# A decoder trunk's even mixer: another order for input blocks, conv taps, padded queries and two modulation groups

## What is computed

```python
z = h @ W['w_in_even'][e]                      # (520, 2568)
q, k, v, fl, a, b = jnp.split(z, cuts, axis=-1)   # 512 512 512 8 512 512
logf = log_sigmoid(fl + b_forget)
o_fox = fox_attend(e, q, k, v, logf)           # 8 heads of 64
u = a * sigmoid(b)                             # 512 channels
cv = depthwise_conv(concat([conv_buf, u]), width 31) + conv_b
cv = silu(group_norm(cv) * conv_norm_g + conv_norm_b)
out = concat([o_fox, cv]) @ W['w_out_even'][e]
```

## Time and profile before

| | us |
|---|---|
| median of 3 runs | 1890.92 |
| lowest and highest run | 1886.56, 1895.22 |
| the profiled execution | 1894.45 |
| its span, first to last instruction | 1892.3 |
| PE, DVE, ACT, POOL busy in the span | 1727.2, 896.7, 596.9, 198.2 |
| mean granted TensorE clock | 0.945 of full |

### The profile page before, as it was taken

How to read it: one execution, slowest core, us unless ns; L and a number is a source line. 1 busy time by engine, 2 the same in 40 slices (tenths; PEclk the granted TensorE clock), 3 DMA queues, 4 the chain that set the end, 5 groups by cost and what they waited for, 6 DMA issues and landing times.

```text
span 1892.3 us, 33709 instructions
## 1 busy us (share of the span) xinstructions
PE 1727.2 (91%) x13817; PEld 1561.8 (83%) x13817; DVE 896.7 (47%) x1470; ACT 596.9 (32%) x880; POOL 198.2 (10%) x172
## 2 busy tenths in 40 slices
PE   4798877889899999998999999999959899999997
PEld 3698744449899999998978788798629899999996
DVE  3429588764533233225517546347463533333234
ACT  2333234443432222223324333324322432222222
POOL 1006560001000000001001101001120100000001
PEclk7799767899999999998999999999979999999998
DMA  8946654546636237335323517225736133333321
GB/s 249 273 132 193 185 153 120 168 127 156 168 89 184 84 89 180 89 96 138 95 79 121 197 56 228 90 78 182 235 134 167 57 96 94 89 89 90 90 69 55
DMA packets 368714, 248.96 MB, mean 132 GB/s; under 512 B 9768, under 2 KB 338888, under 8 KB 368591
## 3 DMA queue, kind: packets, MB, share of 16 engines
q1 hardware_dynamic: 333716, 197.04, 37.0%
q0 software_dynamic: 9296, 33.82, 5.1%
q10 hardware_dynamic: 25587, 16.45, 2.9%
HBM read 224.05 MB, written 23.70 MB: 131 GB/s over the span
## 4 chain that ended last, share of the span: by engine, by line
PE 76%; DVE 11%; DMA 3%; ACT 3%; issue 2%; POOL 2%; SPq 1%; ACTq 1%; POOLq 0%; DVEq 0%
PE product L824 56%; PE product L839 6%; DVE CV L1904 2%; POOL sqa L2364 2%; DMA raw<-in_ada_w 2%; PE job L1269 2%; PE job L1252 1%; PE job L715 1%; PE job L1186 1%; DVE SC L1918 1%; PE job L1169 1%; PE product L1017 1%; DVE w_lo L1775 1%; PE job L774 1%; PE product L1112 1%
## 5 line engine op out<-in xcount | busy, mean ns | idle before, releaser
L824 PE MATMUL product<-H_hi,w_lo 128*128 128x260 f32 x2368 | 671.9, 284 | 3.2 <-ACT gate L1301 3.1
L824 PE MATMUL product<-H_hi,w_hi 128*128 128x260 f32 x2368 | 670.1, 283 | 0.0
L824 PE MATMUL product<-H_lo,w_hi 128*128 128x260 f32 x2368 | 669.6, 283 | 0.0
L824 PEld LDWEIGHTS product<-H_hi,w_lo 128*128 128x128 f32 x2368 | 447.0, 189 | 4.5 <-issue 2.5
L824 PEld LDWEIGHTS product<-H_lo,w_hi 128*128 128x128 f32 x2368 | 447.1, 189 | 1.4
L824 PEld LDWEIGHTS product<-H_hi,w_hi 128*128 128x128 f32 x2368 | 447.6, 189 | 0.0
L1775 DVE TENSOR_TENSOR w_lo<-raw,w_hi 128x1024 fp32r<-128x1024 f32 (+1 forms) x228 | 278.4, 1222 | 188.5 <-ACT w_hi L1301 187.9
L1301 ACT ACTIVATE w_hi<-raw 128x1024 fp32r<-128x1024 f32 (+1 forms) x228 | 234.9, 1037 | 254.5 <-PE product L824 188.4
L824 PE MATMUL product<-G_hi,w_lo 128*128 128x260 f32 x880 | 250.6, 285 | 2.8 <-DVE G_lo L1784 1.5
L824 PE MATMUL product<-G_hi,w_hi 128*128 128x260 f32 x880 | 249.8, 284 | 0.0
L824 PE MATMUL product<-G_lo,w_hi 128*128 128x260 f32 x880 | 249.6, 284 | 0.0
(11 more groups left out here) (329 smaller groups left out, 2175.0 us busy)
## 6 DMA issues: line engine op xcount, KB each, us to landing
spare<-in_ada_w SPq DMA_DIRECT2D x48, 512.0 KB, 7.3
raw<-in_w_in_odd SPq DMA_DIRECT2D x48, 512.0 KB, 3.9
raw<-in_w_ffn_gate SPq DMA_DIRECT2D x44, 512.0 KB, 4.2
raw<-in_w_ffn_up SPq DMA_DIRECT2D x44, 512.0 KB, 3.8
kp<-in_cache_k SPq DMA_DIRECT2D x64, 256.0 KB, 2.8
raw<-in_w_ffn_down SPq DMA_DIRECT2D x32, 512.0 KB, 4.7
st<-in_state_ret POOLq DMA_DIRECT2D x28, 512.0 KB, 4.7
out_ret_sample<-st POOLq DMA_DIRECT2D x28, 512.0 KB, 5.1
```

What stands on the lines that cost most here:

```text
L824: mm = pe.matmul(Gp[slot][:, c, 0:CH], w[:, j, k, :], x[:, k, cols], start=k == 0 and p == 0, stop=k == kt - 1 and p == 2)
```

## The change

It reorders the even mixer's work; nothing is computed otherwise.

- **Input blocks.** Channel tile 0's a and b blocks become blocks 0 and 1, the queries 2 to 5, the other a and b blocks 6 to 11. `qs` and `qb` move two blocks later (`QS_AT` 6, `QB_FROM` 8).
- **Taps.** 23 taps of channel tile 0 run in iterations 3 to 8, none in 9 to 14, one in each of 15 to 19; 12 more stand before the first four row maxima (`EARLY_TAPS`). Tiles 0 and 1 are done one tap after the other, each waiting for the one before; tiles 2 and 3 alternate as before. The taps end at step 28 instead of 30. Sample taps come one tile at a time (`SAMPLE_AT`).
- **Dots.** None in iteration 9 but two, then four an iteration instead of 3.5; 42 before the attention instead of 39, the rest in 8 steps instead of 9.
- **Padded queries.** Three buffers for each parity; the first three are made in iteration 19, and in step x the query of x + 5 is padded before the exponential of x + 4, not after the division.
- **The first scores.** TensorE makes scores 0 to 3 before the transposes `ks`, `vn` and `vs`; ACT evicts those after the first four exponentials.
- **Modulation groups 6 and 7.** Their site in the projection (`("in", 0)`: eight loads on SP, two site products, two turns) goes; groups 6 to 9 run as 16 `ada_block`s in steps 0 to 11, two a step from step 8 on (`ada_before`), loaded by ACT.
- **Buffers.** `wf_lo`, `rows_site` and `rows_late` move or change use.

```diff
 ADA_FIRST = 4
-ADA_MID = 8
+ADA_MID = 6
...
 ADA_LATE = 20
-RAW_GROUPS = (0, 1, 2, 3, 8, 9)
-SPARE_SITES = ((("norm", 0), 4), (("in", 0), 6), (("norm", 1), 10), (("gu", 0), 12), (("gu", 1), 14), (("gu", 2), 16),
+RAW_GROUPS = (0, 1, 2, 3, 6, 7, 8, 9)
+SPARE_SITES = ((("norm", 0), 4), (("norm", 1), 10), (("gu", 0), 12), (("gu", 1), 14), (("gu", 2), 16),
...
 SITE_OF = {name: (i + 1, first) for i, (name, first) in enumerate(SPARE_SITES)}
-Q_AT, AB_AT, K_AT, V_AT = 0, 4, 12, 16
-IN_COLUMNS = ([P * j for j in range(4)] + [c for j in range(4) for c in (1544 + P * j, 2056 + P * j)]
+Q_AT, K_AT, V_AT = 2, 12, 16
+AB_COLUMNS = [(1544 + P * j, 2056 + P * j) for j in range(4)]
+IN_COLUMNS = ([*AB_COLUMNS[0]] + [P * j for j in range(4)] + [c for pair in AB_COLUMNS[1:] for c in pair]
...
 def a_block(t):
-    return AB_AT + 2 * t
+    return 4 + 2 * t if t else 0
 def b_block(t):
-    return AB_AT + 2 * t + 1
-QS_AT, QB_FROM, CS_AT, CUM_AT, CUMT_AT = 4, 6, 14, 15, 17
+    return a_block(t) + 1
+QS_AT, QB_FROM, CS_AT, CUM_AT, CUMT_AT = 6, 8, 14, 15, 17
+A_TILE = {a_block(t): t for t in range(4)}
+B_TILE = {b_block(t): t for t in range(4)}
+SAMPLE_AT = {4: 0, 10: 1, 12: 2, 14: 3}
 def dots_before(m):
-    return sum(3 + i % 2 for i in range(9, m))
+    return min(m - 9, 1) * 2 + 4 * max(m - 10, 0) if m > 9 else 0
...
     return min(NPG, dots_before(20) + 3 * x)
-DOT_STEPS = 9
+DOT_STEPS = 8
+TAPS_AT = {3: 2, 4: 3, 5: 5, 6: 5, 7: 5, 8: 3, **{m: 1 for m in range(15, 20)}}
+IN_TAPS = sum(TAPS_AT.values())
+EARLY_TAPS, TAP_END = [IN_TAPS + i for i in (6, 8, 10, 12)], 28
+def taps_before_step(x):
+    done = EARLY_TAPS[-1] + 2 * min(x, DOT_STEPS)
+    late = 4 * CW - EARLY_TAPS[-1] - 2 * DOT_STEPS
+    return done + (late * min(x - DOT_STEPS, TAP_END - DOT_STEPS) // (TAP_END - DOT_STEPS) if x > DOT_STEPS else 0)
 def taps_before(m):
-    return sum(2 - i % 2 for i in range(10, m))
-TAP_END = 30
-def taps_before_step(x):
-    done, late = taps_before(20) + 2 * min(x, DOT_STEPS), 4 * CW - taps_before(20) - 2 * DOT_STEPS
-    return done + (late * min(x - DOT_STEPS, TAP_END - DOT_STEPS) // (TAP_END - DOT_STEPS) if x > DOT_STEPS else 0)
+    return sum(n for i, n in TAPS_AT.items() if i < m)
 LT_AT, CC_AT, MT_AT, MB_AT, EXP_AT, DN_AT, VALUES_AT = 2, 8, 10, 11, 12, 14, 15
-ADA_TURN_AT = {5: 8, 9: 9}
+ADA_TURN_AT = {5: 6, 9: 7, 11: 8, 13: 9}
+ADA_TAKE_AT = {4: 6, 8: 7, 10: 8, 12: 9}
+def ada_before(x):
+    return min(16, x + max(0, x - 8))
...
                     rows_of("qs", QT)
-                if QS_AT <= m < QS_AT + 2:
-                    site_products(("in", 0), only=(m - QS_AT,))
...
                     rows_out("kn", m - V_AT, KT)
-            rows_of("ks", KT)
-            pe.wait_ge(slot_act, in_a + 20)
-            for b in range(TB):
-                rows_out("vn", b, VT)
-            rows_of("vs", VT)
...
                 pe.wait_ge(qz_ready, x + 1)
-                pe.matmul(bank[:, 0:n], qz2[h % 2][x % 2][:], KT[:, h // 2, NB:NB + n], start=True, stop=False)
+                pe.matmul(bank[:, 0:n], qz2[h % 2][q % 3][:], KT[:, h // 2, NB:NB + n], start=True, stop=False)
...
                 scores(x)
+            rows_of("ks", KT)
+            pe.wait_ge(slot_act, in_a + 20)
+            for b in range(TB):
+                rows_out("vn", b, VT)
+            rows_of("vs", VT)
...
                     scores(x + TB)
-                if x < 8:
-                    ada_block(4 * ADA_MID + x)
+                for i in range(ada_before(x), ada_before(x + 1)):
+                    ada_block(4 * ADA_MID + i)
...
                 stage_out(("kn", b), P, 512, A["k_prompt"][0, 0, b * P:(b + 1) * P].rearrange("p h d -> p (h d)"))
+            def pad_queries(x):
+                h, q = x // TB, x % TB
+                rows_ = slice(HD * (h % 2), HD * (h % 2) + HD)
+                if x >= 3:
+                    wait_job(act, ("s", x - 3))
+                n.up(f(qz2[h % 2][q % 3][rows_, :], QT[rows_, h // 2, NB + q * P:NB + (q + 1) * P], ACT.Copy), qz_ready)
...
                     ahead(m + 2)
+                if m == 19:
+                    act.wait_ge(rows_zero, 2)
+                    for x in range(3):
+                        pad_queries(x)
...
                 product_done(m)
-                if AB_AT <= m < K_AT and m % 2 == 1:
-                    t = (m - AB_AT) // 2
+                if m in B_TILE:
+                    t = B_TILE[m]
...
                     n.up(f(halves(gate[:, t % 2, :]), slot(m), ACT.Sigmoid), slot_act)
-                elif AB_AT <= m < K_AT:
-                    n.up(f(halves(AT[:, (m - AB_AT) // 2, :]), slot(m), ACT.Copy), slot_act)
-                elif m < AB_AT:
-                    n.up(f(halves(QT[:, m, :]), slot(m), ACT.Copy, scale=FOX_SCALE), slot_act)
+                elif m in A_TILE:
+                    n.up(f(halves(AT[:, A_TILE[m], :]), slot(m), ACT.Copy), slot_act)
+                elif Q_AT <= m < Q_AT + 4:
+                    n.up(f(halves(QT[:, m - Q_AT, :]), slot(m), ACT.Copy, scale=FOX_SCALE), slot_act)
...
             stage_keys(TB - 1)
-            stage_out("ks", NB, 512, A["k_sample"][0, :, 0].rearrange("p h d -> p (h d)"))
-            for b in range(TB):
-                wait_job(act, ("vn", b))
-                n.up(f(VN[:, b, :], Jp[jobs.bank(("vn", b))][:, :], ACT.Copy), emptied["A"])
-                n.own(emptied["A"])
-                store(act, A["v_prompt"][0, 0, b * P:(b + 1) * P].rearrange("p h d -> p (h d)"), VN[:, b, :], v_stored)
-            stage_out("vs", NB, 512, A["v_sample"][0, :, 0].rearrange("p h d -> p (h d)"))
...
                 n.up(f(w, w, ACT.Copy, scale=ri[:, x:x + 1]), p_ready)
-            def pad_queries(x):
-                h, q = x // TB, x % TB
-                rows_ = slice(HD * (h % 2), HD * (h % 2) + HD)
-                if x % (2 * TB) >= 2:
-                    wait_job(act, ("s", x - 2))
-                elif x >= 2 * TB:
-                    wait_job(act, ("s", x - 2 * TB + 2))
-                n.up(f(qz2[h % 2][x % 2][rows_, :], QT[rows_, h // 2, NB + q * P:NB + (q + 1) * P], ACT.Copy), qz_ready)
-            act.wait_ge(rows_zero, 2)
             for x in range(TB):
-                pad_queries(x)
+                if x < 2:
+                    pad_queries(x + 3)
                 exps(x)
-            pad_queries(TB)
+            stage_out("ks", NB, 512, A["k_sample"][0, :, 0].rearrange("p h d -> p (h d)"))
+            for b in range(TB):
+                wait_job(act, ("vn", b))
+                n.up(f(VN[:, b, :], Jp[jobs.bank(("vn", b))][:, :], ACT.Copy), emptied["A"])
+                n.own(emptied["A"])
+                store(act, A["v_prompt"][0, 0, b * P:(b + 1) * P].rearrange("p h d -> p (h d)"), VN[:, b, :], v_stored)
+            stage_out("vs", NB, 512, A["v_sample"][0, :, 0].rearrange("p h d -> p (h d)"))
...
                        ACT.Copy), emptied["A"])
+                if x + TB + 1 < STEPS:
+                    pad_queries(x + TB + 1)
...
                     divide(x + 2)
-                if x + TB + 1 < STEPS:
-                    pad_queries(x + TB + 1)
-                if x in (4, 8):
-                    take_rows(ADA_MID + x // 4 - 1)
-                if 1 <= x < 5:
-                    load_ada(4 * ADA_MID + x + 3)
+                if x in ADA_TAKE_AT:
+                    take_rows(ADA_TAKE_AT[x])
+                for i in range(ada_before(x - 1), ada_before(x)) if x else ():
+                    if i + 4 < 16:
+                        load_ada(4 * ADA_MID + i + 4)
...
                 cw = vec[:, V_CW + w * 4 + t:V_CW + w * 4 + t + 1]
-                n.own(conv_step, back=1)
+                n.own(conv_step, back=1 if t >= 2 else 0)
...
                 n.up(o, conv_step)
-            taps = [(t, w) for p in range(2) for w in range(CW) for t in (2 * p, 2 * p + 1)]
+            taps = [(t, w) for t in range(2) for w in range(CW)] + [(t, w) for w in range(CW) for t in (2, 3)]
...
                     low_rows(qs2, "qs", 0)
-                if m in (7, 9, 11, 13):
-                    t = (m - 7) // 2
+                if m - 2 in B_TILE:
+                    t = B_TILE[m - 2]
...
                     n.up(v.tensor_tensor(US[:, t, :, CW - 1], AT[:, t, 0:NB], gate[:, t % 2, 0:NB], ALU.mult), u_ready)
-                if m == 9:
-                    for g in site_groups(("in", 0)):
-                        ada_mod(g)
-                    wait_job(dve, ("adr", site_groups(("in", 0))[1]))
-                    dve.wait_ge(pad_ready, 1)
-                    n.own(u_ready)
-                if m == 13:
...
                     for e in range(2):
-                        for i in range(2):
+                        for i in range(3):
...
                     low_rows(cum2, "cumT", 1)
-                if m >= 9:
-                    spread(range(dots_before(m), dots_before(m + 1)), range(taps_before(m), taps_before(m + 1)))
-                if m in (13, 14):
-                    for t in (2 * (m - 13), 2 * (m - 13) + 1):
```

(14 more changed lines are left out.)

24 lines of the change are left out of this document (5 added, 19 removed).

## The result

The changed kernel takes 1879.1 us in the median of six runs (1874.1 to 1885.6), the kernel before beside it 1890.6 (1886.5 to 1895.2): a ratio of 0.9945, 95% interval 0.9926 to 0.9964. Run once more unedited, it gave 0.9951 (0.9930 to 0.9972). It is faster by 0.5%, about 10.5 us, where 18 were forecast. The profiled execution took 1877.74 us, among the faster of its six, and the only profile of the kernel before took 1894.45, 3.5 us above that kernel's median, so the two spans differ by 16.5 us where the medians differ by 11.5.

A forecast was written before the change was run, and what follows sets the result against it. It took TensorE, then DVE, to bound the projection, DVE the early attention, value pages the later. -16.2 + 0.8 + 0.7 - 3 = -17.7 us on 1894.45 gave 1876.8, or 1873 on the median; 8-in-10 range 1861 to 1886.

The forecast's parts named there:

- Part 1: Projection, to the end of block 19: -16.2 us, bounds -16.7 and -3, from removed site products and the `lf` wait.
- the 0.5 us: End of block 15 in the projection: what remains of TensorE's wait for `lf`, put at 0.5 us.
- DVE's sum of 32.7 us: Blocks 10 to 15: splits, dots, gated products, sample taps and `lf` on DVE take 32.7 us, so `lf` comes at 175.6.
- GpSimd's own sum: Blocks 10 to 15: 22 products from 137.2 on, then a last dot and split, put `lf` between 173 and 186 us.
- my middle price of 1.74: GpSimd's products in the projection: 1.74 us each, top of the pace within a run, between 1.53 and 2.09.
- the rival on GpSimd's pace: Projection: products at 1.9 us each hold it, 42 of them ending at 217; 1883 us in all, chance 0.13.
- Part 2: Last projection block to first transpose of probabilities: 23.1 us against 22.3 today, +0.8, bounds -2.1 and +3.6.
- The lag: Behind block 19: DVE is free only 2.9 us later, at 207.5, because GpSimd must first make 42 products.
- Part 3: Attention steps 0 to 14, bounded by DVE: +0.7 us, bounds -3.4 and +7.8, from dots, taps, sums, `ada` blocks and loads.
- The sentence weighed against it: Loads in steps 7 to 10: ACT and SP transfers share 16 engines, giving an estimated +1 us for the 3 taken.
- Part 4: Attention steps 15 to 31: -3 us, bounds 0 and -9, from value pages nearer SP's pace and fewer taps.
- The other side: Rival, projection blocks 3 to 8: taps beside the queries pace TensorE, +8 us, 1899 in all; chance 0.07.

## Why the prediction was right, and where its steps failed

The direction and the range held; the size was right in no step that carried it, except by parts that offset each other.

**Part 1 fell short: -9.9 us in the profile compared, -8.4 on the mean of eight, for -16.2.** The two site products and their turns went, as priced: block 15 ended at 176.2, forecast 177.1. The step that failed is the 0.5 us that I took for what is left of the wait for `lf`, with nothing for what follows it: the wait was 3.3 us. I let DVE's sum of 32.7 us stand alone. From its split at 141.10 to the end of `lf` at 179.38 DVE took 38.3: its dots waited 4.8 us for products, and `lf` lasted 1.26 instead of 0.19. So `lf` came 3.8 us late. GpSimd's own sum missed it too, though not by its price: the 22 products began at 135.49, and the dot of the last ran at 174.07, 1.75 us each, next to my middle price of 1.74, by which my sum gives `lf` at 177.9 (137.2 + 22 x 1.74 + 2.4). But behind that dot I put 2.4 us, for a dot and a split. In my own order a sample tap and `lf` stand there as well, and the whole took 5.3.

The second half of the miss: I priced a short wait by its own length. A wait of 3.3 us left the sums at 4.40 and the next block at 8.1, much as the wait of 7.3 had the earlier trace rows; the clock was at half for 10.2 us instead of 13.7. With `lf` there in time, the run with one line moved ended block 19 where I had put it, but by errors that offset: block 15 ended 1.1 us sooner than I had it (176.05), and block 16 took 7.5 us instead of 5.76, without any wait. The time lies between the forecast and the rival on GpSimd's pace (1883), which had the right engine: 42 products took from 135.49 to 211.46, 1.81 each for its 1.9. But up to the end of block 19 they reach TensorE through `lf` alone: in the run with `lf` sooner they took 1.70 each (135.47 to 206.88), and TensorE was never idle there.

**Part 2's sum was right by chance** (23.3 for 23.1). The lag was 1.3 us and not 2.9, while one tap took 5.05 us and the others some 0.77, where three beside GpSimd were to cost 1.3 each. That nothing is gained from the removed pads held for the reason given: row maxima behind taps. (With `lf` sooner the lag was 2.9: the last dot ended at 207.6, block 19 at 204.7.) What I did not see is that taps, products and evictions can all leave this stretch, which then takes 6.2 us.

**Part 3** was forecast 0.7 up and came out 0.5 down and 0.7 up in the two profiles. Its terms were read from sums and not separated. TensorE waited for `raw` four times, 4.6 us in all for 3, at 0.9 to 1.4 each. The sentence weighed against it, from the Trainium skill, DMA: Bandwidth & Descriptors, section "Issuing engines are not separate DMA queues", would have made that 1 us, an estimate; the pair of 292.49 and 292.50 fits what it says of interleaving, and the total here lay above my figure.

**Part 4** gave 4.5 and 2.5 us for 3. Its cause stays open. The run that put 20 taps back shows that taps pay in the whole (5.9 us), but most of it before step 15: this stretch took 92.4 us there, against 88.7 to 91.2 in the profiles with the changed kernel's taps, and 88.9 in the run with 12 more taps in steps 8 to 27. The padded queries' place is excluded (88.7).

**The other side** fell as argued: five taps took 3.90 us in blocks 5 to 7, 0.78 each, against the 0.99 from which they would have paced TensorE, which stayed at 36.00 of 36. The Trainium skill, VectorE: DVE Perf Modes, section "The DRAIN you can't avoid", measured on copies that a semaphore between them costs nothing extra; with the interleaved taps' 0.66 that is an estimate of 3.3 us for the five, and the trace differs. (The section also says that an operation that nothing holds starts earlier, which I left out.)

**Open.** Row max 12 to 19 took 31.7 to 39.1 us in versions whose steps there are nearly alike. How soon the attention began does not order them: the first turns came at 231.5 and 231.2 us in the longest (37.6 and 39.1), and at 229.6 in the shortest, the run with `lf` sooner (31.7). TensorE's waits for `raw` are longest there (6.0 and 7.2 us; 2.9 to 5.2 in the others), but neither spreading the blocks nor holding the w_out loads shortened it for certain. In their profiles that stretch took back most of what the evictions had gained (3.0 to 4.5 of 5.3 us) and more than the hold on GpSimd had (4.6 to 6 for 3.6); the 6 us of `lf` sooner did show in the whole.

## What to carry to other kernels

When two engines feed one wait, follow the slower feeder's path to the end: what stands behind its last item counts (5.3 us here for 2.4), and the two engines' waits for each other come on top of either sum. A wait that was merely shortened kept most of the low clock behind it (10.2 us of 13.7), and 3.4 us of it were there without any wait. At a seam between two stages, look at what each engine does while another holds the path: here taps, evictions and products all stood in one gap of 23 us, and moving them a few steps on, together with `lf` one block sooner, was worth 18 us, more than the change itself.

## What the runs showed of the hardware

DVE instructions can be held by GpSimd products that run back to back, for longer than one of them: a tap of 0.75 us took 5.05, until 0.56 us behind the end of the third product, and a copy of 0.17 us took 4.43 to 4.55 in seven profiles, until the third product ended. With GpSimd held until the fourth row maximum, no DVE instruction of that stretch took longer than alone. In the profiles with the held copy only the indirect load ran on GpSimd when the copy began, so the load seems to hold it as well; no run shows the load without products behind it. Dots beside such products keep to 0.67 to 0.69 us. The Trainium skill, SBUF — State Buffer, section "Who interferes with whom", says that a VectorE instruction with two SBUF inputs contends with a GpSimd instruction that reads SBUF, that a copy can in a mode that uses both ports, and that a reduction does not; the runs agree in which are held. It gives the ports to one engine for one instruction, and here three passed. In the projection a tap beside products takes 1.15 to 1.47 us, up to 1.82 with `lf` sooner; why no more pass it there is not shown.

The granted clock can be at its lower level without a wait of TensorE ahead of it: in the run with `lf` sooner it was 0.50 from 178.3 to 181.7 us, behind 20 matmuls of 128x8 (2.29 us) and no idle time.
